# Rotary partners fetched by on-chip transfers instead of rotation products, in a kernel of ten mixers and MLPs

## What is computed

```python
def apply_rope(t, cos, sin):                       # even mixer, heads of 64
    t1, t2 = tf[..., :HEAD_DIM // 2], tf[..., HEAD_DIM // 2:]
    return jnp.concatenate([t1 * c - t2 * s, t2 * c + t1 * s], axis=-1)
...
def apply_axial_rope(x, cos, sin):                 # second mixer, heads of 64, and 32 of the other kind
    rot = lambda z: jnp.concatenate([-z[..., q:], z[..., :q]], axis=-1)
    x_rot = jnp.concatenate([rot(xr), rot(xc)], axis=-1)
    return x * c + x_rot * s
```

## Time and profile before

| | |
|---|---|
| median of 3 runs (3440.70 to 3442.33) | 3442.33 us |
| the profiled execution | 3441.55 us |
| its span, first to last instruction | 3439.70 us |
| busy: PE / PEld / DVE / ACT / POOL | 99 / 80 / 61 / 44 / 58% of the span |
| TensorE's granted clock, mean of the span | 0.998 of full |

### The profile page before, as it was taken

How to read it: one execution, slowest core, us unless ns; L and a number is a source line. 1 busy time by engine, 2 the same in 40 slices (tenths; PEclk the granted TensorE clock), 3 DMA queues, 4 the chain that set the end, 5 groups by cost and what they waited for, 6 DMA issues and landing times. The chain is left out here.

```text
span 3439.7 us, 46281 instructions
## 1 busy us (share of the span) xinstructions
PE 3400.9 (99%) x17572; PEld 2761.2 (80%) x17572; DVE 2087.8 (61%) x2990; ACT 1530.3 (44%) x2388; POOL 1989.7 (58%) x2338
## 2 busy tenths in 40 slices
PE   9999999999999999999999999999999999999999
PEld 8888868888888888748888887788788876888887
DVE  5556666655764468766645667326767575238667
ACT  4334454333533355675333537434444555335444
POOL 6555645555655658745665557554655665546564
PEclk9999999999999999999999999999999999999999
DMA  4223203233222322202332220123222210232321
GB/s 173 89 77 117 85 20 118 79 110 111 86 98 91 130 70 93 71 1 83 123 111 103 83 76 26 56 92 123 98 98 92 86 59 8 93 105 92 114 107 62
DMA packets 87726, 301.56 MB, mean 88 GB/s; under 512 B 9936, under 2 KB 14544, under 8 KB 87120
## 3 DMA queue, kind: packets, MB, share of 16 engines
q1 hardware_dynamic: 85392, 296.50, 24.4%
q10 hardware_dynamic: 2112, 2.10, 0.2%
HBM read 296.46 MB, written 2.10 MB: 87 GB/s over the span
## 5 line engine op out<-in xcount | busy, mean ns | idle before, releaser
L408 POOL TENSOR_TENSOR w_lo<-w_raw,w_hi 128x256 fp32r<-128x256 f32 x1754 | 1364.6, 812 | 1091.5 <-ACT w_hi L381 841.9
L419 PE MATMUL bank<-xh,w_hi 128*128 128x512 f32 x2544 | 997.8, 392 | 3.9 <-issue 1.5
L421 PE MATMUL bank<-xh,w_lo 128*128 128x512 f32 x2544 | 989.2, 389 | 0.0
L420 PE MATMUL bank<-xl,w_hi 128*128 128x512 f32 x2544 | 989.2, 389 | 0.0
L381 ACT ACTIVATE w_hi<-w_raw 128x1024 fp32r<-128x1024 f32 (+2 forms) x485 | 498.5, 1039 | 671.3 <-DMA w_raw<-in_ffn_up 269.3
L419 PEld LDWEIGHTS bank<-xh,w_hi 128*128 128x128 f32 x2544 | 478.1, 188 | 106.5 <-issue 4.6
L420 PEld LDWEIGHTS bank<-xl,w_hi 128*128 128x128 f32 x2544 | 478.2, 188 | 99.7 <-issue 2.4
L421 PEld LDWEIGHTS bank<-xh,w_lo 128*128 128x128 f32 x2544 | 478.0, 188 | 99.5
L408 POOL TENSOR_TENSOR extra_lo<-extra_raw,w_hi 128x256 fp32r<-128x256 f32 x264 | 229.8, 905 | 126.1 <-ACT w_hi L381 113.1
L1099 DVE TENSOR_TENSOR y_tok<-y_tok,bank 128x512 f32<-128x512 f32 x232 | 157.4, 685 | 223.1 <-PE bank L978 223.1
L1133 DVE TENSOR_TENSOR work<-bank,sqsum 128x512 f32<-128x512 f32 x88 | 60.7, 690 | 267.7 <-PE bank L421 267.7
(11 more groups left out here) (454 smaller groups left out, 6154.2 us busy)
## 6 DMA issues: line engine op xcount, KB each, us to landing
w_raw<-in_ffn_up SPq DMA_DIRECT2D x176, 512.0 KB, 3.5
w_raw<-in_b_ffn_up SPq DMA_DIRECT2D x64, 512.0 KB, 3.5
extra_raw<-in_ffn_down SPq DMA_DIRECT2D x52, 512.0 KB, 4.5
w_raw<-in_b_gates SPq DMA_DIRECT2D x48, 512.0 KB, 3.4
extra_raw<-in_b_ffn_down SPq DMA_DIRECT2D x40, 512.0 KB, 4.5
w_raw<-in_od_in SPq DMA_DIRECT2D x33, 512.0 KB, 3.5
w_raw<-in_b_in SPq DMA_DIRECT2D x24, 512.0 KB, 3.6
w_raw<-in_ffn_down SPq DMA_DIRECT2D x20, 512.0 KB, 3.4
```

The costliest lines, as they stand in the source:

```text
L408: ins = pool.tensor_tensor(lo_of(g, part), raw_of(g, part), hi_of(g, part).bitcast(F32), ALU.subtract)
L419: pe.matmul(out, wh, hi, start=first, stop=False)
L420: pe.matmul(out, wh, lo, start=False, stop=False)
L421: return pe.matmul(out, wl, hi, start=False, stop=last)
```

## The change

The rotation tiles are no longer PE's. `EVEN_TILES` and `TILES2` leave them out, so PE's list is shorter by eight products in each of the three stages, and all later tiles fall on other banks. In their place ACT issues transfers from SBUF to SBUF that fetch the partner rows into a buffer with two slots (`partner`, which lies in `work`, and `b_partner`): four of 32 rows x 512 for most, eight of 16 rows for kr and the two rotup. In the second mixer the features are ordered anew on the host (`turned_order`) so that partners lie 32 or 16 rows apart; the signs are moved into the sine tables. DVE multiplies the fetched rows by the sine, where it read PSUM before. ACT waits before it issues: for the tile itself, and from the third rotation on until DVE has finished the rotation that used the same slot. DVE waits for the transfers' semaphore (`partner_moved`).

```diff
+EVEN_TILES = [item for item in EVEN_ORDER if item[0] != "rot"]
...
-        raw = work[:, 2:6, :]
+        raw, partner = work[:, 2:6, :], work[:, 6:8, :]
...
         def even_pe(pe, c, e):
...
-                elif kind == "rot":
-                    pe.wait_ge(acc_drained, acc_free(tile))
-                    pe.wait_ge(raw_copied, c.at("raw") + i - 2 + 1)
-                    pe.wait_ge(tables_loaded, 48)
-                    pe.matmul(out, e_tab[:, 2432:2560], raw[:, i % 4, :], start=True, stop=True).then_inc(side_done, 1)
...
         def even_act(act, c):
...
                     act.activation(raw[:, i % 4, :], bank[(c.tiles + n) % ACCS][:], ACT.Copy).then_inc(raw_copied, 1)
+                    act.wait_ge(raw_copied, c.at("raw") + i - 1)
+                    if i >= 4:
+                        act.wait_ge(rotated, i - 3)
+                    for to in range(4):
+                        at = to + 1 - 2 * (to % 2)
+                        act.dma_start(partner[32 * to:32 * to + 32, i % 2, :], raw[32 * at:32 * at + 32, i % 4, :])\
+                           .then_inc(partner_moved[i % 2], 16)
...
         def even_dve(dve, ch, c):
...
+                if kind == "rot":
+                    dve.wait_ge(partner_moved[i % 2], 64 * (i // 2))
+                    ch.link(dve.tensor_tensor(tmp[:, i % 2, :], partner[:, i % 2, :], e_tab[:, S:2 * S], ALU.mult))
+                    dve.tensor_tensor(e_qk[:, i - 2, :], e_qk[:, i - 2, :], tmp[:, i % 2, :], ALU.add)\
+                       .then_inc(rotated, 1)
...
-        STEPS2 = ("sum", "add")
+        STEPS2 = ("sum", "add", "rot", "rotkr", "rotup")
...
+        MOVE_AT = {("rot", 0): ("qk", 1), ("rot", 1): ("qk", 2), ("rot", 4): ("qk", 3), ("rot", 2): ("kr", 0), ("rotkr", 0): ("va", 0),
+                   ("rot", 3): ("va", 0), ("rotup", 0): ("upr", 1), ("rotup", 1): ("upn", 0)}
...
         def mix2_act(act, c, layer):
...
+            def move(r):
+                src, made = rotated_tile(*ROTS2[r])
+                wide = HD // 2 if ROTS2[r][0] == "rot" else 16
+                act.wait_ge(acc_drained, drained(T + TILES2.index(made)))
+                if r >= 2:
+                    act.wait_ge(rotated, c.at("rotated") + r - 1)
+                for to in range(0, P, wide):
+                    at = to + wide if to // wide % 2 == 0 else to - wide
+                    act.dma_start(b_partner[to:to + wide, r % 2, :], src[at:at + wide, :]).then_inc(partner_moved[r % 2], 16)
...
+                for r, item in enumerate(ROTS2):
+                    if MOVE_AT[item] == (kind, i):
+                        move(r)
...
         def mix2_dve(dve, ch, c):
...
+                    if kind == "rot" and i < 4:
+                        ch.link(dve.scalar_tensor_tensor(out=work[:, 0, :], in0=b_partner[:, r % 2, :], scalar=b_small[:, 7:8],
+                                                         in1=b_tab[:, SIN_A:SIN_A + S], op0=ALU.mult, op1=ALU.mult))
...
-                    ch.link(dve.tensor_scalar(b_rot[:], b_tab[:, ROT_A:ROT_A + P], b_small[:, 0:1], None, ALU.mult))
```

More of the change, by code:

```diff
@@ L292, in build @@
         side_done, raw_copied, rotated = sem("side_done"), sem("raw_copied"), sem("rotated")
+        partner_moved = [sem(f"partner_moved{i}") for i in range(2)]
         tables_loaded, odd_loaded = sem("tables_loaded"), sem("odd_loaded")
@@ L1421, in even_end @@
             c.blocks += 20
-            c.tiles += len(EVEN_ORDER)
-            c.add("side", 12)
+            c.tiles += len(EVEN_TILES)
+            c.add("side", 4)
             c.add("raw", 8)
@@ L1481, in even_act @@
             g = c.blocks
-            for n, (kind, i) in enumerate(EVEN_ORDER):
+            for n, (kind, i) in enumerate(EVEN_TILES):
                 if kind in ("lin", "val"):
@@ L1494, in even_act @@
             k = c.copy()
-            k.tiles += len(EVEN_ORDER)
+            k.tiles += len(EVEN_TILES)
             out_act(act, k, 1, c.blocks + 12, y)
@@ L2207, in mix2_end @@
             c.tiles += len(TILES2)
-            c.add("side", SIDES2 + len(ROTS2))
+            c.add("side", SIDES2)
             c.add("rotated", len(ROTS2))
@@ L2291, in mix2_pe @@
                     mm.then_inc(side_done, 1)
-                elif kind in ("rot", "rotkr", "rotup"):
-                    src, made = rotated_tile(kind, i)
-                    turn = b_rot[:] if kind == "rot" and i < 4 else b_tab[:, ROT_A:ROT_A + P] if kind == "rot" else \
-                        b_tab[:, ROT_B:ROT_B + P]
-                    pe.wait_ge(acc_drained, acc_free(tile))
-                    pe.wait_ge(acc_drained, drained(c.tiles + TILES2.index(made)))
-                    pe.wait_ge(tables_loaded, 48 + 32 * (c.at("tables") + 1))
-                    pe.matmul(out, turn, src, start=True, stop=True).then_inc(side_done, 1)
                 elif kind in ("upr", "upn"):
@@ L2399, in mix2_act @@
                 n += 1
-                if (kind, i) == ("rotup", 0):
+                if (kind, i) == ("upn", 1):
                     act.wait_ge(rotated, c.at("rotated") + ROTS2.index(("rot", 3)) + 1)
@@ L2833, in even_table, with turn_sign, turned_order @@
     pool = np.concatenate([np.repeat(inv_count[0:2], HD, 0), np.repeat(inv_count[2:4], HD, 0)], 1)
-    return np.concatenate([np.cos(ang), np.sin(ang), mask, pool, rotation(P, HD)], 1).astype(f)
-def rotation(n, width, first=0):
-    r = np.zeros((n, n), np.float32)
-    for p in range(first, n):
-        low = (p - first) % width < width // 2
-        r[p + (width // 2 if low else -width // 2), p] = -1 if low else 1
-    return r
+    return np.concatenate([np.cos(ang), turn_sign(HD) * np.sin(ang), mask, pool], 1).astype(f)
+def turn_sign(width):
+    return np.where(np.arange(P) % width < width // 2, -1, 1)[:, None]
+def turned_order(dim):
+    return np.arange(dim).reshape(2, 2, dim // 4).transpose(1, 0, 2).reshape(-1)
 def second_table():
@@ L2854, in angles @@
         return np.concatenate([r, r, c, c], 1).T.astype(f)
-    a, b = np.tile(angles(HD), (2, 1)), angles(32)
+    a, b = np.tile(angles(HD)[turned_order(HD)], (2, 1)), angles(32)[turned_order(32)]
     b = np.tile(b, (4, 1))
-    return np.concatenate([np.cos(a), np.sin(a), np.cos(b), np.sin(b), rotation(P, 32), rotation(P, 16)], 1).astype(f)
+    return np.concatenate([np.cos(a), turn_sign(HD) * np.sin(a), np.cos(b), turn_sign(32) * np.sin(b)], 1).astype(f)
 def lay_out(a):
@@ L2911, in lay_out @@
     a_cols = np.concatenate([np.arange(HD) + HD * head for j in range(4) for head in (j, j + 4)])
+    order_a, order_b = turned_order(HD), turned_order(32)
+    q_cols = np.concatenate([order_a + HD * head for j in range(4) for head in (j, j + 4)])
+    k_cols = np.concatenate([512 + order_a + HD * head for head in range(2)])
     ins, ups, kvs, gates, outs, smalls, fup, fdown = ([] for _ in range(8))
```

81 lines of the change are left out of this document (40 added, 41 removed).

## The result

The changed kernel takes **3456.19 us** (median of 5 runs, 3454.92 to 3460.16), the kernel before, timed beside it, 3442.24 (5 runs): ratio 1.0041, 95% interval 1.0031 to 1.0052. The forecast was 3436.0 with a range of 3426 to 3447 and a chance of 0.16 for slower. It is 14 us slower, although 48 passes have gone from TensorE. The profiled execution has a span of 3453.1 us.

What follows compares the result with a forecast made beforehand. The prediction took TensorE, busy 99% of the span, as the bound. 0.2 us from the even mixer plus 2 x 2.7 from the second mixers made 5.6 off 3441.55, giving 3436.0 us, range 3426 to 3447.

Steps and rivals of the forecast that it cites:

- What is removed: All three stages: 24 rotation products at 0.9 us leave TensorE, 21.6 us in all, 7.2 for each stage.
- Even mixer, TensorE's side: TensorE stands 5.2 us ahead of lin 6 and loses 1.8 to the clock: 7.2 - 5.2 - 1.8 = +0.2 us.
- Even mixer, VectorE's side: Lateness of 7.0 us against 7.6 idle before value tile 1, so VectorE ends about where it did.
- Second mixer: Issues delay the square root and last rotations; attention keeps 3.6 of 7.2 us, less 0.9 clock: 2.7 for each mixer.
- I take 0.4: ScalarE's queue: each of the 120 added issues takes 0.4 us, with bounds 0.33 and 0.53.
- The nearest rows: Basis for issue time: SP's stores of 128 rows, 0.33 to 0.45 us, and ScalarE's loads, median 0.53.
- Expensive issues: Rival: issues at 0.6 us make ScalarE's queue the limit of both stages, 3449.2 us; chance 0.18.
- Cheap issues: Rival: a 32-row transfer issues in 0.25 us or less, or beside the running rounding, 3427.0 us; chance 0.24.
- Serial transfers: Rival: a queue's transfers don't overlap, eight land 14.4 us after the first issue, 3476 us; chance 0.04.
- All kept: Rival: rotation wait and issues both hidden, so all 21.6 us are kept, 3420.0 us; chance 0.04.

Runs made afterwards that it cites:

- pair_no_add: pair_all without the additions of the 24 rotations (VectorE's last operation of each), output then lacking the sine part: 3421.42 us (0.9940).
- round_first: The changed kernel with rotation 4's issues moved behind the five roundings of lin 5's step instead of ahead of them: 3452.45 us (1.0033).
- Four_slots: The changed kernel with four partner slots instead of two, in the even mixer alone: 3450.70 us (1.0026).
- sp_queue: The changed kernel with the same 120 transfers and two slots, issued by SP instead of ScalarE: 3443.07 us (1.0003).
- mix2_only: The change in the two second mixers only; the even mixer keeps the rotation products of the kernel before: 3450.71 us (1.0025).
- one_wide: two_wide with one transfer of all 128 rows per partner tile, 24 issues, so rotations get the wrong partner: 3436.0 us (0.9982).
- two_wide: The changed kernel with partners in neighbouring rows, two transfers of 64 rows per partner tile, 48 issues instead of 120: 3436.46 us (0.9985).
- pair_all: two_wide with four slots in the even mixer, roundings ahead of rotation 4's issues, and VectorE's casts moved behind rotation 3: 3433.64 us (0.9974).

## Why the forecast was wrong

**What is removed: not contradicted.** 48 passes are gone, and the run without VectorE's additions (pair_no_add) lies 21.2 us below the kernel before, near the 21.6 summed, but it has less work for VectorE than either kernel. No run isolates the passes.

**Even mixer, TensorE's side: right.** Forecast: roundings from 401.2, a stand of 5.2 us, 1.8 us of clock. Measured: 401.46, 5.35, and twelve passes that follow by 0.43 instead of 0.23, 2.4 us.

**Even mixer, VectorE's side: the step that failed.** "So VectorE ends about where it did." It drains value tile 1 at 447.49 in place of 442.51, and TensorE stands 4.4 us for it. The 3.4 us of lateness at lin 5 were right (3.47). They grow to 9.6, where the sum had 7.0: 8.3 us at the split of the second pooling group, for the copy of lin 9 stands behind issues that wait for an earlier rotation, and that group's rounding behind four issues more; and 1.3 from the casts at value tile 0 (0.65 each in place of 0.23). The larger error is the slack. I set 7.6 us of idle time against it, but the 2.96 ahead of lin 7 were not free, and 2.54 of them are still there. Two things hold back the copy that VectorE waits for (419.87, before 415.40). TensorE, which I had just made 5 us late, is late with lin 7 as well: its last pass starts at 418.88, before at 414.97. And ScalarE gets to the copy only behind rotation 6's issues, which wait for VectorE's own rotation 4, and a rounding; this ends last, and in round_first it holds the copy 2 us longer than TensorE does. Only the waits ahead of the value tiles, 1.34 + 3.34, took lateness up: 9.6 - 4.7 = 4.9. Behind that stand the clock was at 0.83 and 0.91 of full for the next 40 us, 5.2 us at full speed lost, of which a part lies in the stand itself. Four_slots, round_first and sp_queue each take a part of ScalarE's lateness away, and the stage comes back to +3.4, +2.3 and +0.3.

**Second mixer: mechanism right, one term mis-sized.** "I take 0.4": an issue takes 0.61, over the upper bound of 0.53. The forecast's own rival had the rule, 28 issues on the path of each mixer: 28 x 0.21 = 5.9, 2.7 - 5.9 = -3.2. Measured: -2.7 and -2.9 in the trace, 4 each in mix2_only; the attention starts 5.5 us later behind kr's tile than forecast. The rest of the path has the forecast's order: square root, reciprocal, kr's rotation (3.0 in place of 2.3), rotations that wait for a transfer (2.04 and 1.16 us for the two rotup), then TensorE, first for a bank and then for kn 3. The nearest rows misled: SP's stores of 128 rows, which still take 0.42 here. ScalarE's own first loads, 0.53, were nearer.

**The rivals.** Expensive issues came true in the second mixers and gave 3449.2 for the whole; the missing 7 us are VectorE's side of the even mixer. Cheap issues: wrong in price, though an issue does run beside the rounding ahead of it, which the earlier trace rows, where the issues came first, could not show. Serial transfers: no. Eight are issued within 5.0 us, and these transfers land a median 2.1 and at most 4.7 after their own issue, not 14.4 after the first. The rule of the Trainium skill (SBUF — State Buffer, "Can I just issue two DMAs to hit both halves?"), that two transfers to different partitions serialize, does not show at this size. All kept: not even with 24 issues in place of 120 (one_wide, 3436.0).

**What is shown, what is argued, what is open.** Shown: that the loss against the kernel before is ScalarE's queue (sp_queue, with the same transfers and banks; two_wide); that behind it VectorE holds the saving back (pair_no_add; in sp_queue VectorE waits for nothing from lin 2 to the turns). Argued from single rows: how the 9.6 us of lateness are made up, and what takes the slack ahead of lin 7. Open: why an issue behind another is dearer, how much exactly of pair_no_add's 12 us is clock, and why the first second mixer loses 8.6 us in mix2_only.

## What to carry to other kernels

A transfer is paid in the queue that issues it, by the piece: choose a layout that needs two wide transfers and not eight narrow ones before asking what moves the data. Before a saving on the busiest engine is booked, check the next engine's slack at each place, and do not count as slack an idle time that only exists because the engines ahead of it are on time. Where a short stand can't be avoided, idle products ahead of it keep the clock, but this pays only if nothing behind it is late for another reason; here the version with two transfers, four slots, reordered roundings, earlier casts and fillers (pair_filled) takes 3425.9 us, 0.46% less than before.

## What the runs showed of the hardware that was not expected

- An on-chip transfer of 16 or 32 rows x 512 takes 0.51 us to issue as the first of a group and 0.61 behind another, on ScalarE (0.51 and 0.59 on SP). With 64 rows, every second one, it is 0.47 and 0.62, and 0.47 for one of 128 rows by itself (two_wide, one_wide). SP's 512 KB loads take 0.33.
- An issue starts 0.06 to 0.1 us after the start of a 1.06 us rounding ahead of it; an instruction behind it waits until it is through.
- After TensorE stood 5.35 us the next twelve passes followed by 0.43 us (1.2 GHz for most of them; the granted clock of 400 to 420 is 0.83) and then by 0.23; with 40 idle passes of 128 x 128 and a stand of 0.9 they followed by 0.23 from the second on.
- The same kernel can differ by 10 us and more from run to run (two_wide 3430.8 to 3442.5, at mean granted clocks of 0.998 and 0.993) where it has stands of 2 to 4 us in several stages; pair_all spreads over 10, and with its stands filled up over 2.3 (pair_filled).
